# A modulation phase rebuilt: tokens turned before W_ada arrives, W_ada in four column blocks, low parts shared out anew

## The reference

```python
mod_x = (silu_c @ w_ada[l] + b_ada[l])[:, None, :]
mod_c = silu_cc @ w_ada[l] + b_ada[l]
sh1x, sc1x, gt1x, sh2x, sc2x, gt2x = jnp.split(mod_x, 6, axis=-1)
hx = rmsnorm(x, norm1_g[l]) * (1.0 + sc1x) + sh1x
hc = rmsnorm(xc, norm1_g[l]) * (1.0 + sc1c) + sh1c
...
p = h @ w_in
```

## Time and profile before

| | us |
|---|---|
| median of three runs | 1803.25 |
| profiled execution | 1795.54 |
| its span | 1793.5 |
| PE busy in the span | 1572.9 (88%) |
| DVE busy | 1011.8 (56%) |
| ACT busy | 641.6 (36%) |
| POOL busy | 425.6 (24%) |
| mean granted clock of PE | 0.951 |

### The profile page before, as it was taken

The page is one execution under the profiler, slowest core; times in us unless marked ns, Lnnn a source line. Parts: engine busy times, 40 slices in busy tenths (PEclk is TensorE's granted clock), DMA queues, the critical chain, the costliest instruction groups (busy, mean ns, idle before and its releaser), DMA issues. The chain is left out here.

```text
span 1793.5 us, 35173 instructions
## 1 busy us (share of the span) xinstructions
PE 1572.9 (88%) x15022; PEld 1325.9 (74%) x15022; DVE 1011.8 (56%) x1542; ACT 641.6 (36%) x976; POOL 425.6 (24%) x376
## 2 busy tenths in 40 slices
PE   4599999999966888878776798789999989899997
PEld 1366887999966777777775587568888867787876
DVE  2534553101104776777776755845545588887975
ACT  3366435221102222232222223455545543333333
POOL 1301111111112455555554311323223200000000
PEclk7799999999987998999998899899999999999999
DMA  7213424426543543333322232034453487163422
GB/s 307 75 53 97 120 69 123 133 85 197 172 121 90 151 125 100 112 113 108 108 62 66 94 126 98 24 123 136 153 170 130 156 317 256 63 235 109 173 83 94
DMA packets 169565, 229.81 MB, mean 128 GB/s; under 512 B 34189, under 2 KB 101121, under 8 KB 168386
## 3 DMA queue, kind: packets, MB, share of 16 engines
q1 hardware_dynamic: 162562, 205.79, 35.2%
q0 software_dynamic: 6848, 21.76, 3.8%
HBM read 165.78 MB, written 61.73 MB: 127 GB/s over the span
## 5 line engine op out<-in xcount | busy, mean ns | idle before, releaser
L87 PE MATMUL fps<-xh_m,w1r_hi 128*128 128x512 f32 x448 | 177.6, 396 | 18.9 <-ACT s L2321 5.4
L87 PE MATMUL fps<-bh,ah 128*128 128x512 f32 x448 | 176.4, 394 | 13.6 <-DVE acc L2636 9.1
L88 PE MATMUL fps<-xl_m,w1r_hi 128*128 128x512 f32 x448 | 176.7, 394 | 0.0
L89 PE MATMUL fps<-xh_m,w1r_lo 128*128 128x512 f32 x448 | 176.5, 394 | 0.0
L89 PE MATMUL fps<-bh,al 128*128 128x512 f32 x448 | 176.0, 393 | 0.0
L88 PE MATMUL fps<-bl,ah 128*128 128x512 f32 x448 | 175.8, 392 | 0.0
L80 PE MATMUL ps_main<-hhi,whi 128*128 128x512 f32 (+3 forms) x360 | 136.4, 379 | 15.7 <-DVE wlo L647 11.8
L82 PE MATMUL ps_main<-hhi,wlo 128*128 128x512 f32 (+3 forms) x360 | 132.8, 369 | 0.0
L81 PE MATMUL ps_main<-hlo,whi 128*128 128x512 f32 (+3 forms) x360 | 132.7, 369 | 0.0
L2283 ACT ACTIVATE ah<-araw 128x2048 fp32r<-128x2048 f32 x28 | 53.7, 1918 | 186.4 <-PE fps L89 120.7
L80 PE MATMUL ps_main<-whi,hhi 128*128 128x256 f32 x416 | 120.0, 288 | 0.0
(11 more groups left out here) (307 smaller groups left out, 3596.6 us busy)
## 6 DMA issues: line engine op xcount, KB each, us to landing
s_hid<-hb SPq DMA_DIRECT2D x112, 256.0 KB, 2.3
araw<-s_hid SPq DMA_DIRECT2D x28, 1024.0 KB, 6.6
w1raw<-in_w_ff SPq DMA_DIRECT2D x16, 1024.0 KB, 6.2
w2b<-in_w_ff SPq DMA_DIRECT2D x16, 1024.0 KB, 6.2
raw<-in_w_in SPq DMA_DIRECT2D x14, 1024.0 KB, 5.2
wa<-in_w_ada SPq DMA_DIRECT2D x8, 1024.0 KB, 10.5
z_sb<-in_w_ada SPq DMA_DIRECT2D x16, 512.0 KB, 4.5
n_sb<-in_w_ada SPq DMA_DIRECT2D x16, 512.0 KB, 4.3
```

The costliest lines, as they stand in the source:

```text
L87: pe.matmul(out, lhi, rhi, start=start, stop=False, skip_group_check=True)
L88: pe.matmul(out, lhi, rlo, start=False, stop=False, skip_group_check=True)
L89: return pe.matmul(out, llo, rhi, start=False, stop=stop, skip_group_check=True)
```

## The change

The modulation is written anew, and the small unit of the projections is moved into it.

- The tokens are loaded first, W_ada after them. W_ada comes in four blocks `g` of 256 shift columns and 256 scale columns (two transfers of 1 MB each, in pieces of 1 KB), in two slots. Block `g` holds what the feature tiles 2g and 2g+1 need. After each block its columns are complete: eight products (`columns`), a copy out by ACT (`row`), four small products (`select`), two DVE operations (`scales`).
- The tiles are not multiplied by `rstd`. DVE makes a diagonal matrix of it (`diagonal`), and PE multiplies each 128x128 block of tokens with it (`turn`), which turns and scales at once. These are plain fp32 products, not transposes. DVE copies tiles 0 to 5 out of PSUM into `xt`, ACT tiles 6 to 9 (`turned`).
- Scale and shift are then applied in place in SBUF in eleven pieces (`full`), seven by DVE and four by ACT; ACT rounds all eleven (`high`); POOL makes the low parts of pieces 1, 3, 5 and 7, DVE the other seven (`low`).
- The small unit of W_in is loaded behind W_ada and split at the end of the modulation. `project_phase` has it ready (`K.ws_hi`, `K.ws_lo`) and begins with its products, while unit 1 is loaded and split.

The diff, added lines of the modulation first (those removed stand in the kernel above), then the projection:

```diff
+        NG, W = 4, 2 * P
+        SLOTS = 2
+        TOGETHER = ((0, 1), (1, 1), (2, 2), (4, 2), (6, 2), (8, 2))
+        xt = m.sb("xturn", [P, KT, NTOK])
+        wa = m.sb("wa", [P, SLOTS, KT, 2, W])
+        diag = m.sb("diag", [P, 4, P])
...
+        HALF = 512
+        PIECES = [(0, 0, HALF), (1, 0, HALF), (0, HALF, NTOK), (1, HALF, NTOK), (2, 0, NTOK), (3, 0, NTOK), (4, 0, NTOK),
+                  (5, 0, NTOK), (6, 0, NTOK), (7, 0, HALF), (7, HALF, NTOK)]
+        BY_ACT = (1, 3, 5)
+        T_ACT = 6
...
+            xr = [A["x"][t * P:(t + 1) * P, :] for t in range(TL)] + [A["ctx"][t * P:(t + 1) * P, :] for t in range(TC)]
+            sp.dma_start(xs[:, 0], xr[0]).then_inc(ld_x[0], 16)
+            for t in range(1, 4):
+                sp.dma_start(xs[:, t], xr[t]).then_inc(ld_x[t], 16)
+            for t in range(4, NT):
+                sp.dma_start(xs[:, t], xr[t]).then_inc(ld_x[t], 16)
+            wv = A["w_ada"].rearrange("(p k) (z n) -> p z k n", k=KT, n=D)
+            def load_w(g):
+                if g >= SLOTS:
+                    sp.wait_ge(w_used, g - SLOTS + 1)
+                for z in range(2):
+                    sp.dma_start(wa[:, g % SLOTS, :, z], wv[:, z, :, g * W:(g + 1) * W]).then_inc(ld_w[g % SLOTS], 16)
+            for g in range(NG):
+                load_w(g)
+            wi = A["w_in"].rearrange("(k p) n -> p k n", p=P)
+            sp.wait_ge(wpad_done, 1)
+            sp.dma_start(wraw[:, :, 0:16], wi[:, :, OFF_R:OFF_R + 16]).then_inc(ld_small, 16)
...
+            def turned(t):
+                for h in range(2):
+                    act.wait_ge(t_ready, 2 * t + h + 1)
...
+            def row(g):
+                act.wait_ge(w_used, g + 1)
+                if g:
+                    act.wait_ge(mod_ready, g)
+                act.activation(modrow[:].rearrange("p z j n -> p (z j n)"), ps_row[:], ACT.Copy).then_inc(row_done, 1)
+            def full(x):
+                k, lo, hi = PIECES[x]
+                act.wait_ge(sc1_done, k // 2 + 1)
+                if hi > HALF:
+                    act.wait_ge(t_act, 2 * (NT - T_ACT))
+                act.wait_ge(t_dve, 2 * T_ACT)
+                full_piece(act, lambda a, s, b: act.activation(a, a, ACT.Identity, scale=s, bias=b), x, hf_act)
+            def high(x):
+                k, lo, hi = PIECES[x]
+                act.wait_ge(hf_act if k in BY_ACT else hf_dve, fulls(x))
+                act.activation(K.hhi[:, k, lo:hi], xt[:, k, lo:hi], ACT.Copy).then_inc(hi_done, 1)
...
+            row(0)
+            turned(6)
+            turned(7)
+            full(1)
+            high(0)
+            high(1)
+            turned(8)
+            turned(9)
+            row(1)
+            full(3)
+            high(2)
+            high(3)
+            row(2)
+            full(5)
+            high(4)
+            high(5)
+            row(3)
+            full(7)
+            high(6)
+            high(7)
+            high(8)
+            act.wait_ge(ss_done, NT)
+            high(9)
+            high(10)
+            act.wait_ge(ld_small, 32)
+            act.activation(K.ws_hi[:], wraw[:], ACT.Copy).then_inc(small_hi, 1)
...
+            def diagonal(r):
+                t0, n = TOGETHER[r]
+                dve.wait_ge(rstd_done, r + 1)
+                if r == 0:
+                    dve.wait_ge(ld_const, 16)
+                for t in range(t0, t0 + n):
+                    if t >= 4:
+                        dve.wait_ge(t_ready, 2 * (t - 3))
+                    dve.tensor_scalar(diag[:, t % 4], K.ident[:], rstd[:, t:t + 1], None, ALU.mult).then_inc(diag_done, 1)
+            def turned(t):
+                for h in range(2):
+                    dve.wait_ge(t_ready, 2 * t + h + 1)
+                    dve.tensor_copy(xt[:, features(h), tokens(t)],
+                                    ps_t[:, 2 * (t % 2) + h].rearrange("p (k n) -> p k n", n=P)).then_inc(t_dve, 1)
+            def scales(g):
+                if g == 0:
+                    dve.wait_ge(cols_done, 1)
+                ks = slice(2 * g, 2 * g + 2)
+                dve.wait_ge(mod_ready, g + 1)
...
+            def full(x):
+                k, lo, hi = PIECES[x]
+                if hi > HALF:
+                    dve.wait_ge(t_act, 2 * (NT - T_ACT))
+                dve.wait_ge(t_dve, 2 * T_ACT)
+                full_piece(dve, lambda a, s, b: dve.tensor_scalar(a, a, s, b, ALU.mult, ALU.add), x, hf_dve)
+            def low(x):
+                k, lo, hi = PIECES[x]
+                dve.wait_ge(hi_done, x + 1)
+                dve.tensor_tensor(K.hlo[:, k, lo:hi], xt[:, k, lo:hi], K.hhi[:, k, lo:hi].bitcast(F32),
+                                  ALU.subtract).then_inc(lo_done, 1)
+            variance(0)
+            diagonal(0)
+            variance(1)
+            diagonal(1)
+            turned(0)
...
+            turned(5)
...
+            diagonal(5)
+            scales(0)
+            full(0)
+            low(0)
+            full(2)
+            scales(1)
+            full(4)
+            low(2)
+            scales(2)
+            full(6)
+            low(4)
+            scales(3)
+            full(8)
+            full(9)
+            full(10)
+            for x in (6, 8, 9, 10):
+                low(x)
+            dve.wait_ge(small_hi, 1)
+            dve.tensor_tensor(K.ws_lo[:], wraw[:], K.ws_hi[:].bitcast(F32), ALU.subtract)
...
+            for x in (1, 3, 5, 7):
+                k, lo, hi = PIECES[x]
+                pool.wait_ge(hi_done, x + 1)
+                pool.tensor_tensor(K.hlo[:, k, lo:hi], xt[:, k, lo:hi], K.hhi[:, k, lo:hi].bitcast(F32), ALU.subtract)
...
+            def turn(t):
+                pe.wait_ge(diag_done, t + 1)
+                if t >= 2:
+                    pe.wait_ge(t_dve, 2 * min(t - 1, T_ACT))
+                if t - 2 >= T_ACT:
+                    pe.wait_ge(t_act, 2 * (t - 1 - T_ACT))
+                for h in range(2):
+                    for i in range(4):
+                        k = 4 * h + i
+                        last = pe.matmul(ps_t[:, 2 * (t % 2) + h, i * P:(i + 1) * P], xs[:, t, k * P:(k + 1) * P],
+                                         diag[:, t % 4], start=True, stop=True)
+                    last.then_inc(t_ready, 1)
+            def columns(g):
+                pe.wait_ge(ld_w[g % SLOTS], 32 * (g // SLOTS + 1))
+                if g:
+                    pe.wait_ge(row_done, g)
+                for k in range(KT):
+                    q = slice(32 * (k % 4), 32 * (k % 4) + 32)
+                    last = pe.matmul(ps_row[q, :], K.csil[:, k, :], wa[:, g % SLOTS, k].rearrange("p z n -> p (z n)"),
+                                     start=(k < 4), stop=(k >= 4))
+                last.then_inc(w_used, 1)
+            def select(g):
+                pe.wait_ge(row_done, g + 1)
...
+                for z in range(2):
+                    for j in range(2):
+                        c = 8 * g + 4 * z + 2 * j
+                        last = pe.matmul(both[g % 2][:, c:c + 2], modrow[:, z, j], sel2[:], start=True, stop=True)
+                last.then_inc(mod_ready, 1)
+            for t in range(5):
+                turn(t)
+            pe.wait_ge(ld_rows, 4 * 16)
+            pe.wait_ge(ld_const, 16)
+            pe.transpose(ps_cols[:, :100], rows[:100, :], K.ident[:100, :100]).then_inc(cols_ready, 1)
+            turn(5)
+            columns(0)
+            turn(6)
+            select(0)
+            turn(7)
+            turn(8)
+            turn(9)
+            for g in range(1, NG):
+                columns(g)
+                select(g)
...
-                if u >= 2:
-                    sp.wait_ge(lo_done, u - 1)
-                if kind == "small":
-                    sp.dma_start(raw[:, u % 2, :, 0:16], wv[:, :, OFF_R:OFF_R + 16]).then_inc(ld_w[u % 2], 16)
-                    sp.dma_start(raw[:, u % 2, :, 32:48], wv[:, :, OFF_AB:OFF_AB + 16]).then_inc(ld_w[u % 2], 16)
-                else:
-                    sp.dma_start(raw[:, u % 2], wv[:, :, col:col + width]).then_inc(ld_w[u % 2], 16)
+                if u >= 3:
+                    sp.wait_ge(lo_done, u - 2)
+                sp.dma_start(raw[:, u % 2], wv[:, :, col:col + width]).then_inc(ld_w[u % 2], 16)
...
+            load_unit(1)
+            sp.dma_start(wlr[0:RANK, :], A["gla_w_lr"].rearrange("z r n -> r z n")).then_inc(ld_s, 16)
...
+            for u in range(2, NU):
                 load_unit(u)
...
-            act.wait_ge(init_done, 3)
-            split(0)
+            act.wait_ge(init_done, 2)
             split(1)
...
-            pe.wait_ge(init_done, 3)
...
-                        last = mm3(pe, ps_main[:width, i % 3, :n], whi[:, b, k, :width], wlo[:, b, k, :width],
+                        last = mm3(pe, ps_main[:width, i % 3, :n], K.ws_hi[:, k], K.ws_lo[:, k],
                                    K.hhi[:, k, t0:t0 + n], K.hlo[:, k, t0:t0 + n], k == 0, k == KT - 1)
```

(31 more changed lines are left out.)

214 lines of the change are left out of this document (66 added, 148 removed).

## The result

The changed kernel took 1782.06 us (median of 4 runs, 1781.42 to 1788.34), beside 1802.99 us of the kernel before in the same comparison: a ratio of 0.9891 [0.9868, 0.9914]. I had predicted 1790.7 and a range from 1785 to 1798. The profiled execution took 1788.34 us, its span 1786.6.

What follows compares the result with a forecast made beforehand. The prediction took the kernel to be bound by when PE starts the projections: 62.5 instead of 75.06 us, 12.5 less. Taken from the timed median, 1803.25 - 12.5 = 1790.7 us, range 1785 to 1798.

Steps and rivals of the forecast that it cites:

- What decides: Whole kernel: the gain is PE's earlier start of the projections, 12.5 us; later phases move as a whole.
- The turns: Modulation, token turning on PE: turns 0 to 5 run from 7.5 to 21.3 us, before block 0 lands.
- C: Rival, token turns: longer at half clock, turns 0 to 5 end at 28.4, gain 6.3, 1797 us; chance 0.14.
- E: Rival, modulation: PE never gets full clock, start at 77.9, kernel 1806 to 1809 us; chance 0.06.
- D's price: Rival, turns: products cost four transposes, a turn 6.0 us, 3.0 at full clock, kernel 1801; chance 0.03.
- D's factor: Same rival, chance 0.03: fp32 product against transpose, four times supposed; forecast read 2.3 from 0.43 against 0.19.
- Block 0: Modulation, first W_ada block: 5.6 us at 380 GB/s after the tokens land at 16.5, so landed at 22.2.
- The columns: Modulation, a block's eight column products on PE: 3.9 us at half clock, 2.1 at full.
- Block 3: Modulation, last W_ada block: load issued at 36.4 when block 1's slot is free, landing 7.9 to 8.0 later, 44.4.
- The tail: Modulation's end: columns 3.9, copy 0.6, selection 1.88, scales 0.55, then 2.0 + 3.0 (POOL in full) + 4.6 + 0.6, to 61.6.
- Rival B: Modulation's tail lighter: full clock for block 3 (2.7 less) or POOL's piece covered (3.0 less), 1785 to 1788; chance 0.22.
- The failed step: Whole kernel: 12.5 us taken off the timed median 1803.25, 7.7 above the profiled execution, giving 1790.7.

Runs made afterwards that it cites:

- e3: Kernel before with only the small unit's load and split moved into the modulation, and the changed projection: 1790.21 us, ratio 0.9970 to the kernel before.
- e4: Changed modulation without the small unit's load and split, with the projection of the kernel before: 1791.74 us, ratio 0.9982 to the kernel before.
- e1: The changed kernel run again unchanged, beside the kernel before: 1785.48 us, ratio 0.9947.
- e9: The changed kernel run a third time unchanged, beside the kernel before in another group: 1784.40 us, ratio 0.9931.
- e5: Changed kernel with POOL's last low part (piece 7) given to DVE: 1785.63 us, ratio 0.9930 to the kernel before.
- e6: Changed kernel with all eleven low parts on DVE, none on POOL: 1783.86 us, ratio 0.9917 to the kernel before.

## Why the prediction was right in its mechanism and wrong in its time

**What decides.** "The change is worth what it does to one moment: when PE starts the projections." Borne out in the main: e3 and e4 move that moment by 6.9 and 2.9 us and the median by 5.9 and 4.3. "Every later phase ... is moved as a whole" is not: see the sum over the phases below.

**The turns.** Forecast from 7.5 to 21.3; they ran from 7.66 to 21.39. Half clock lasted until 12.93, a turn and a half, where I had given it the first turn alone. That the end fits all the same is partly chance: the forecast followed DVE's order, and here PE worked without a pause. Rivals C and E needed half clock for all six and fell, and D's price too: a later turn takes 1.97, not 3.0. D's factor was misread as well. Of the 16 instructions in 34 to 37 us three are the selection's; 13 are transposes, and their starts lie 0.213 us apart. So a full product, 0.43, costs 2.0 of them at half clock, not 2.3.

**Block 0.** Forecast to land at 22.2, landed at 24.95, 2.75 late. Summed over the windows, 7.5 MB (tokens, constants and block 0) had flowed at about 23.6 us: 1.1 of it because the tokens didn't flow at 420 GB/s from the start, as I had it, and 0.4 because of "I take 380, nearer to the latter" for the 1 KB pieces. The other 1.3 is the spread between the transfer engines: each transfer has sixteen completion signals in the trace, which I read as one of each engine, and those of block 0's second MB come from 23.50 to 24.82. By then some 0.5 MB more than block 0 had flowed, so engines that were done with it went on with block 1. That block 1 holds block 0 up doesn't follow: in e4 block 3 has nothing behind it, and its signals still spread from 47.17 to 48.34. I had let a block land when its bytes had flowed at the mean rate.

**The columns.** Forecast 3.9 at half clock: 1.92 in the first trace, 2.52 to 3.64 in the eight others with the new modulation (3.59 to 3.64 in four of them). In all nine PE had stood idle for 3.6 to 5.0 us before them, and the clock after it varies between executions of one kernel. So half clock was near in most traces, and too long by 2.0 us in the first.

**Block 3.** Forecast 8.0 from the slot's release to its landing; 9.85 (36.96 to 46.81). The windows of that load:

```profile
37.00:38.50 1.50, 0.81 (x8) 0.82 (x8) 0.00 (x0) 1.47 (x3) 0.00 (x0) 1.00 0.08 18
38.50:40.00 1.50, 1.50 (x18) 0.57 (x18) 1.15 (x4) 1.50 (x3) 0.00 (x0) 1.00 0.86 290
40.00:44.00 4.00, 1.65 (x16) 0.97 (x8) 2.71 (x6) 3.63 (x6) 2.49 (x1) 0.96 1.05 356
44.00:45.00 1.00, 0.00 (x0) 0.00 (x0) 0.97 (x2) 1.00 (x2) 0.00 (x0) 0.50 1.27 248
45.00:46.00 1.00, 0.00 (x0) 0.00 (x0) 0.56 (x1) 0.19 (x1) 0.73 (x1) 0.50 0.80 98
```

By 45 us 2.13 MB have flowed (0.03 + 0.44 + 1.42 + 0.25), as many as block 3 has, and at 356 GB/s it would be down at about 44.5. Yet its last piece comes at 46.81, and in 45 to 46 us the transfers are 0.80 busy and carry 98 GB/s. The small unit's loads, 64-byte pieces issued behind block 3, fit that, and e4 tests it: it has the new modulation without these loads. Its block 3, from windows and PE's row:

```profile
40.50:42.00 1.50, 1.50 (x16) 1.03 (x19) 0.56 (x3) 1.50 (x3) 0.00 (x0) 1.00 0.65 197
42.00:46.00 4.00, 2.24 (x20) 1.10 (x12) 2.71 (x6) 3.63 (x6) 2.49 (x1) 1.00 1.04 351
46.00:47.00 1.00, 0.00 (x0) 0.00 (x0) 0.97 (x3) 1.00 (x2) 0.00 (x0) 1.00 1.08 350
47.00:48.00 1.00, 0.00 (x0) 0.00 (x0) 1.00 (x1) 0.79 (x1) 0.14 (x1) 0.53 0.22 74
48.38 3.64 PE L384 MATMUL ps_row<-wa,csil 128*32 128x512 f32 x16 [3.43 <-DMA wa<-in_w_ada]
```

The slot was released at 39.56, so the load took 8.82 here. In the five traces with the small loads behind it and block 1's columns in their old place (first, e1, e9, e5, e6) it took 9.5 to 9.95. The small loads cost 0.7 to 1.1 us, by one trace without them; the rest of the error of 1.85, some 0.8, is there without them too.

**The tail.** From the start of block 3's columns to its scaling, 7.0 forecast and 5.85 measured: "selection 1.88" came out as 1.05 there, and as 1.87 in e9, and the columns took 3.64 for 3.9. "I add POOL's 3.0 in full" was right: DVE ended at 59.77 and POOL 2.74 later. The form was another than I had thought, since POOL's instruction was issued in between and got almost nothing done while DVE worked without a break. The rule of the Trainium skill ("SBUF — State Buffer", section "Who interferes with whom") that the two exclude each other for a whole instruction agrees with both orders seen, 7.38 on POOL or 4.94 on DVE. The DVE instructions held up in the second order are scalings with one input tile in SBUF, for which that page of the Trainium skill says this of the 2-port modes alone; no trace shows whether they ran in one. Rival B had two terms. The covered piece fell; the full clock for block 3's columns did not come (3.64), only its selection of 1.05.

**The start.** The steps' errors, +2.75 - 1.98 - 0.21 + 1.85 - 1.15 - 0.35 + 0.1, make 1.0, and PE started at 63.53 for 62.5. Over the three traces of the changed kernel it started at 65.0 on average, beside 74.8 in two of the kernel before: 9.8 us, not 12.5. So the term was over-sized by 2.7, about what block 0 comes late (landed at 25.1 on average for 22.2).

**Terms that I did not have.** One is the MLP phase, over 1000 us later. Its windows, before and after:

```profile
1111.30:1793.50 682.20, 634.37 (x2752) 519.71 (x2752) 469.07 (x430) 300.90 (x419) 92.06 (x64) 0.97 0.43 149
```

```profile
1106.80:1786.60 679.80, 633.80 (x2752) 519.63 (x2752) 469.12 (x430) 301.00 (x419) 91.25 (x64) 0.97 0.44 150
```

Its busy times agree to 0.8 us on every engine, yet it is 2.4 us shorter. All nine traces with the new modulation have 679.3 to 680.0 there, e4's among them; the three with the old one have 681.7 to 682.2, e3's among them. So it goes with the modulation and not with the projection. What in it does this I can't say. The phase's 1500th product comes 306.1 to 306.9 us into it with the new modulation and 306.5 to 307.4 with the old, the 2000th at 493.9 to 494.6 and 496.3 to 496.8, so nearly all of it arises between them.

Over the three traces of the changed kernel and the two of the kernel before, the means differ by -9.8 at PE's start, +1.3 in the projections, +0.6 in the mix phase, -0.6 in the merge phase and -2.5 in the MLP phase: -11.0, as the spans do (1783.9 beside 1794.9). The middle three are no more than traces with the same code in that phase differ by: e5 and e6 have 461.0 and 461.4 in the projections, where the changed kernel has 462.8 to 463.7. The timed medians say 12.5. That this equals the term of the sum is luck in part: the start was over-sized by 2.7, and what the later phases gave, 1.2 by the traces, was not in it.

**The failed step.** "The median of the timed runs stands 7.7 above it, and I predict it: 1803.25 - 12.5 = 1790.7." The sum made against the profiled execution itself was 1783.0; measured were 1782.06, and 1784.7 in the later runs. The step that failed is the level to which the 12.5 was applied. Three runs that lay together looked like one. Over 63 later runs the kernel before has a median of 1797.2, 6.0 lower, and a spread of 17.6 us, and the profiled execution with 1795.54 was closer to it. With 1797.2 as the level the same sum gives 1784.7. That accounts for 6.0 of the 8.6 us by which the time was missed. The other 2.6 are between the changed kernel's own four runs and its later median. The range was built from the costs of the change alone, and nothing in it stood for how far a few runs can be from the kernel's own median. Why the runs of the kernel before lay high together in the first comparison, and so why the gain came out as 20.9 there, stays open.

**The signs.** Of those named for being wrong none came: no later turn took over 2 us, DVE did not wait for ACT at the end, and unit 1's products followed without a wait. The four blocks' columns came at 24.95, 35.04, 38.67 and 46.81 for 22, 34, 36 to 37 and 44.

## What to carry to other kernels

When the profiled execution and the timed median of a few runs disagree by an amount that matters beside the effect (7.7 beside 12.5 us here), take both as draws of one spread and let the range reach to either. Count transfers by the rate of their own piece size in a long stream, allow for the last of the transfer engines (1.2 to 1.3 us after the first here), and look at what is issued behind them. Where a phase ends in DVE and POOL at elementwise work on SBUF as here, add their times, and give POOL only what stands in time that another wait covers. And of a ring of two slots, use what has landed before other work, since the slot's release is the next transfer's start.
